# The beginning of a two-layer hybrid trunk kernel: normalized tokens made feature first

## What is computed

```python
def _rms_norm(x, g):
    xf = x.astype(jnp.float32)
    y = xf * lax.rsqrt(jnp.mean(xf * xf, axis=-1, keepdims=True) + EPS)
    return (y * g.astype(jnp.float32)).astype(x.dtype)

def _ada(cond, w, b):
    m = jax.nn.silu(cond) @ w + b
    return jnp.split(m, 3, axis=-1)

def _prologue(x, ctx, c, c_ctx, g, w_mod, b_mod):
    sh, sc, gt = _ada(c, w_mod, b_mod)
    shc, scc, gtc = _ada(c_ctx, w_mod, b_mod)
    hx = _rms_norm(x, g) * (1 + sc[:, None]) + sh[:, None]
    hc = _rms_norm(ctx, g) * (1 + scc) + shc
    h = jnp.concatenate([hc, hx], axis=1)
    return h, gt[:, None], gtc
...
    h, gt, gtc = _prologue(x, ctx, c, c_ctx, norm_g, w_mod, b_mod)
    u, v, g_a, xs, g_b = jnp.split(
        h @ w_in, [A_WIDTH, 2 * A_WIDTH, 3 * A_WIDTH, 3 * A_WIDTH + B_WIDTH], axis=-1)
```

## Time and profile before

| | us |
|---|---|
| median of 3 timed runs | 1304.54 (1301.89 to 1306.85) |
| the profiled execution, device time | 1301.15 |
| the profiled execution, span of the core | 1299.3 |
| PE busy with matmuls | 1223.0 (94%) |
| DVE busy | 851.6 (66%) |
| ACT busy | 518.3 (40%) |
| POOL busy | 445.6 (34%) |

### The profile page before, as it was taken

The page is one execution under the profiler, slowest core; times in us unless marked ns, Lnnn a source line. Parts: engine busy times, 40 slices in busy tenths (PEclk is TensorE's granted clock), DMA queues, the critical chain, the costliest instruction groups (busy, mean ns, idle before and its releaser), DMA issues.

```text
span 1299.3 us, 21119 instructions
## 1 busy us (share of the span) xinstructions
PE 1223.0 (94%) x8508; PEld 1079.1 (83%) x8508; DVE 851.6 (66%) x1494; ACT 518.3 (40%) x956; POOL 445.6 (34%) x358
## 2 busy tenths in 40 slices
PE   1799989999999899999999999999999999999997
PEld 1789878888888848999999998877788888888997
DVE  6697956989925253136484899448877877776125
ACT  6632353320015331034524432146666666665012
POOL 0600000000000003332112212139999888988332
PEclk9899999999999999999999999999999999999999
DMA  9614677425422962103211112330000000000402
GB/s 347 241 66 130 153 209 247 148 81 203 162 90 85 324 231 56 64 33 116 70 44 34 33 66 81 111 100 9 9 17 9 17 9 17 17 9 9 162 28 103
DMA packets 87408, 127.99 MB, mean 99 GB/s; under 512 B 12912, under 2 KB 59376, under 8 KB 86512
## 3 DMA queue, kind: packets, MB, share of 16 engines
q1 hardware_dynamic: 77200, 110.81, 25.8%
q10 hardware_dynamic: 10112, 15.85, 3.5%
HBM read 95.71 MB, written 30.93 MB: 97 GB/s over the span
## 4 chain that ended last, share of the span: by engine, by line
PE 78%; DVE 11%; DMA 4%; ACT 3%; POOL 3%; issue 2%; SPq 0%; ACTq 0%; POOLq 0%; DVEq 0%
PE ps L1732 10%; PE ps L1734 10%; PE ps L1733 10%; PE ps L1743 5%; PE ps L1744 5%; PE ps L1745 5%; PE ps L1986 3%; DVE region_d L1008 3%; PE ps L2020 2%; PE ps L2021 2%; PE ps L2022 2%; PE ps L2006 2%; PE ps L2009 2%; PE ps L2008 2%; PE ps L2007 2%; PE ps L1598 2%
## 5 line engine op out<-in xcount | busy, mean ns | idle before, releaser
L1732 PE MATMUL ps<-w_hi,a_hi 128*128 128x256 f32 x896 | 256.6, 286 | 9.9 <-DVE b_lo L1109 6.3
L1733 PE MATMUL ps<-w_lo,a_hi 128*128 128x256 f32 x896 | 254.9, 284 | 0.0
L1734 PE MATMUL ps<-w_hi,c_lo 128*128 128x256 f32 x736 | 208.2, 283 | 0.0
L601 POOL TENSOR_TENSOR region_b<-region_b,region_d 128x256 f32<-128x256 f32 x40 | 29.7, 749 | 510.0 <-DVE region_d L1412 510.0
L1732 PEld LDWEIGHTS ps<-w_hi,a_hi 128*128 128x128 f32 x896 | 173.2, 193 | 12.2 <-issue 3.7
L1733 PEld LDWEIGHTS ps<-w_lo,a_hi 128*128 128x128 f32 x896 | 173.4, 194 | 0.0
L594 POOL TENSOR_TENSOR w_lo<-weight_ring,w_hi 128x2048 fp32r<-128x2048 f32 x16 | 74.0, 4625 | 199.3 <-ACT w_hi L649 199.3
L1734 PEld LDWEIGHTS ps<-w_hi,c_lo 128*128 128x128 f32 x736 | 141.2, 192 | 0.0
L1743 PE MATMUL ps<-a_hi,w_hi 128*128 128x512 f32 (+1 forms) x384 | 138.6, 361 | 1.4 <-ACT region_d L649 1.4
L1508 DVE TENSOR_REDUCE small<-ps 128x1 f32<-128x1280 f32 x64 | 95.2, 1487 | 65.1 <-PE ps L1986 65.1
L1744 PE MATMUL ps<-b_lo,w_hi 128*128 128x512 f32 (+1 forms) x384 | 136.6, 356 | 0.0
(11 more groups left out here) (225 smaller groups left out, 2940.9 us busy)
## 6 DMA issues: line engine op xcount, KB each, us to landing
weight_ring<-in_w_mod SPq DMA_DIRECT2D x10, 2048.0 KB, 8.5
weight_ring<-in_we_in SPq DMA_DIRECT2D x10, 1024.0 KB, 6.0
weight_ring<-in_wo_in SPq DMA_DIRECT2D x10, 1024.0 KB, 5.2
weight_ring<-cop_t_scratch SPq DMA_DIRECT2D x4, 1536.0 KB, 7.9
region_a<-in_x SPq DMA_DIRECT2D x4, 1024.0 KB, 14.4
region_c<-in_w_mod SPq DMA_DIRECT2D x2, 2048.0 KB, 19.3
bop_scratch<-region_d ACTq DMA_DIRECT2D x16, 256.0 KB, 2.6
cop_t_scratch<-region_d SPq DMA_DIRECT2D x8, 512.0 KB, 7.4
```

The source lines that it names most:

```text
L1732: te.matmul(o, th, wh[:, k], start=k == 0, stop=False)
L1733: te.matmul(o, th, wl[:, k], start=False, stop=False)
L1734: last = te.matmul(o, tl, wh[:, k], start=False, stop=k == last_k)
```

## The change

- The host lays the tokens out a second time, feature first (`xt_in`, 128 x 8 x 1280). They are loaded straight into hT0: chunk 0 in one transfer, chunk 1 in two (features 0 to 511 and 512 to 1023) ahead of the weights; chunk 2 in two, behind the second half of the v weights and the third block of w_mod. The first v weights are now loaded ahead of the second w_mod block, and b_in and c_in by SP's queue and not ACT's. The token-first loads, row scalings, 80 transposes and 24 copies of the beginning are gone.
- ACT squares whole chunks (`feature_squares`) into XQ (region_a). PE sums them over features with one-column matmuls (`token_sums`), ACT takes the root of each chunk apart (`token_root`), DVE refines the reciprocal (`token_rstd`), PE spreads it over all partitions by transposing a broadcast column (`rstd_across`), ACT copies it to rstd_rows (region_d; `rstd_copy`).
- POOL multiplies the tokens of chunks 0 and 1 by rstd_rows (`scale_tokens`, three products of 2048 columns), and, for chunk 2, adds the eight blocks of squares in three halving steps, both ahead of its parameter work.
- Chunk 2 is scaled on DVE together with the modulation (`h_last`), and rounded by ACT in `h_round2`.
- DVE's order is another: the exp of the magnitudes and the parity work behind the sine stand behind the low parts of the first feature half and both weights_rest of v. PE does the lower feature halves of six token tiles for both v halves, then the upper ones; `after_v` and `after_xs` have new places for the state-space work. `weights_rest(("xs", 0))` is ahead of `build_cl(0)`, and the last `mod_evac` of layer 0 behind `weights_rest(("xs", 1))`.
- Some semaphores are shared where there were several.

```diff
-        early = [(M[0], 0), (M[1], 1), (("v", 0), 2), (("v", 1), 0), (M[4], 1), (M[5], 1), (("xs", 0), 1), (("xs", 1), 0),
+        early = [(M[0], 0), (("v", 0), 2), (M[1], 1), (("v", 1), 0), (M[4], 1), (M[5], 1), (("xs", 0), 1), (("xs", 1), 0),
...
-        after_v = {1: [("mods", 4)], 2: [("cols", 4)], 5: [("mods", 5)], 6: [("cols", 5), ("xs", 0)], 7: [("bop", 0)], 8: [("bop", 4)],
-                   9: [("lags", 0)]}
-        after_xs = {0: [("xs", 1)], 2: [("bop", 8)], 4: [("ws", 0)], 5: [("lags", 1)], 6: [("gb", 0), ("bop", 12)], 7: [("vg", 0)],
-                    8: [("vg", 5)]}
+        after_v = {1: [("bc", 2)], 2: [("mods", 4)], 3: [("cols", 4)], 5: [("mods", 5)], 6: [("cols", 5)], 7: [("xs", 0), ("bop", 0)],
+                   9: [("bop", 4)]}
+        after_xs = {1: [("xs", 1)], 2: [("lags", 0)], 4: [("bop", 8)], 5: [("ws", 0)], 7: [("lags", 1)], 8: [("gb", 0), ("bop", 12)],
+                    9: [("vg", 0)], 10: [("vg", 5)]}
...
-            token_loads(X, ld_x)
-            ring_load(*M[0])
-            ring_load(*M[1])
-            ring_load("v", 0)
...
+            feature_load(slice(0, KT), 0, ld_x[0])
+            feature_load(slice(0, 4), 1, ld_x[1])
+            feature_load(slice(4, KT), 1, ld_x[2])
+            ring_load(*M[0])
+            ring_load("v", 0)
+            ring_load(*M[1])
             ring_load("v", 1)
+            off_ring_load(2, s_ld_v)
+            feature_load(slice(0, 4), 2, ld_x[3])
+            feature_load(slice(4, KT), 2, ld_x[4])
+            off_ring_load(3, s_ld_ws)
...
+            def scale_tokens(ks, q, n):
+
+                t0, nt = CHUNKS[q]
+                pool.wait_ge(s_bc_ok, q + 1)
+                z = hT0[:, ks, t0:t0 + nt]
+                g.tensor_tensor(z, z, rstd_rows[:, t0:t0 + nt].unsqueeze(1).broadcast_to([P, n, nt]), ALU.mult).then_inc(s_z, 1)
+
+            scale_tokens(slice(0, KT), 0, KT)
+            scale_tokens(slice(0, 4), 1, 4)
+            scale_tokens(slice(4, KT), 1, 4)
+            t0, nt = CHUNKS[2]
+            pool.wait_ge(s_sq, 5)
+            for i, m in enumerate((4, 2, 1)):
+                a, b = XQ[:, 0:m, t0:t0 + nt], XQ[:, m:2 * m, t0:t0 + nt]
+                g.tensor_tensor(a, a, b, ALU.add).then_inc(s_z, 1)
+                pool.wait_ge(s_z, 4 + i)
...
+            feature_squares(0, slice(0, KT), 0)
+            feature_squares(1, slice(0, 4), 1)
+            token_root(0)
+            feature_squares(2, slice(4, KT), 1)
+            token_root(1)
+            rstd_copy(0)
+            weights_round(("v", 0))
+            mod_row(0)
+            rstd_copy(1)
             mod_row(1)
-            raw_evac(1, (0, 2, 3, 5, 6))
-            weights_round(("v", 0))
-            act.wait_ge(s_h_tr, 16)
             h_round(0, 0)
+            h_round(0, 1)
+            weights_round(("v", 1))
             mod_row(2)
-            h_round(0, 1)
-            raw_evac(2, (0, 2, 3, 5, 6))
-            act.wait_ge(s_h_tr, 24)
+            feature_squares(3, slice(0, 4), 2)
+            feature_squares(4, slice(4, KT), 2)
             mod_row(3)
-            h_round(0, 2)
             h_round(1, 0)
             h_round(1, 1)
-            weights_round(("v", 1))
-            h_round(1, 2)
+            token_root(2)
+            rstd_copy(2)
+            h_round2()
...
+            def h_last(ks):
+
+                t0, nt = CHUNKS[2]
+                if ks[0] == 0:
+                    dve.wait_ge(s_bc_ok, 3)
+                for k in ks:
+                    z = hT0[:, k, t0:t0 + nt]
+                    v.scalar_tensor_tensor(out=z, in0=z, scalar=hA[0][:, k, 0:1], in1=rstd_rows[:, t0:t0 + nt],
+                                           op0=ALU.mult, op1=ALU.mult).then_inc(s_z2, 1)
...
+            def token_sums(q, e):
+
+                t0, nt = CHUNKS[q]
+                for i in range(nt // P):
+                    for k in (range(KT) if e is None else range(4 * e, 4 * e + 4)):
+                        last = te.matmul(sums(q)[:, i:i + 1], XQ[:, k, t0 + P * i:t0 + P * i + P], onec, start=k == 0 and i == 0,
+                                         stop=k == KT - 1 and i == nt // P - 1)
+                return last
```

250 lines of the change are left out of this document (140 added, 110 removed).

## The result

| | before | changed |
|---|---|---|
| median of the timed runs, us | 1305.05 | 1325.43 |
| ratio | | 1.0157, 95% interval 1.0127 to 1.0186 |
| profiled execution, us | 1301.15 | 1327.08 |
| span of the core, us | 1299.3 | 1325.3 |
| first v tile | 48.99 | 54.31 |

The forecast was 1310 (1290 to 1317) with 0.45 for no measurable change. The kernel is slower, and the median lies above the range. Both spans are read in three pieces: the first v tile is 5.3 us later, the stretch from there to the gMLP stage takes 173.3 us and not 155.2, and what lies behind takes 1097.7 and not 1095.1. That is 5.3 + 18.1 + 2.6 = 26.0, the difference of the spans.

A forecast was written before the change was run, and what follows sets the result against it. PE's chain of work bounds the kernel, from when the first v tile runs: 44.0 + 147.5 work + 18.1 holes puts the gMLP stage at 209.6, 5.4 later; 1304.54 + 5.4 = 1310 us, range 1290 to 1317.

The forecast's parts named there:

- The sums: PE's one-column token sums before the first v tile: first 16 from 8.7 to 15.4 us, chunk 1's 16 end at about 21.
- From the roots of chunk 1 to the first v tile: VectorE, held by GpSimd's products, then low parts: first v tile at 44.0 instead of 48.99, 5.0 us gained.
- Rival 3: GpSimd's products with a repeated operand cost 1.5 times 4.6 us: 1320 us; decides from 1.25 on; chance 0.12.
- The holes: PE idle between first v tile and gMLP stage: 18.1 us in sum, against 12.7 for break-even and 7.7 before.
- (a): Low parts of chunks 0 and 1, upper features: GpSimd's halving tree holds VectorE's trigonometry; PE hole of 6.7 us.
- (b): At cols(4): ACT has mod_row(4) behind the eight h_round2, which wait on VectorE; PE hole of 5.4 us.
- (c): Second xs slot: later trigonometry and parameters, build_cl(0) done at 138.4; hole near xs tile 4 of 2.0 us (0 to 4).
- (d): End of xs: both chains 14 us later, the work behind them 5; hole of 4.0 us (2.4 to 6).
- PE's work: PE's busy time between first v tile and gMLP stage: 147.5 us as before; 3.65 removed, 2.3 and 1.4 added.
- "Nothing behind it differs": From the gMLP start on: nothing changes, so a start at 209.6 us gives a span of 1304.7.
- Rivals 1 and 2: GpSimd hardly holds VectorE: 1290 us, chance 0.13; holds it by half: 1294 to 1303, chance 0.17.
- rival 4: At the start: sums and roots could still be the gate despite earlier w_mod; counted in the sum, no chance given.

## Why the prediction was wrong

It summed to a span of 1304.7 and the span was 1325.3, 20.6 us more. (In the medians it is 15.4, 1325.43 for 1310; the rest is where the profiled executions lie among the others.) The direction was right, the size not. By its own steps:

1. **The sums (+10.0 us, the step that failed).** The prediction priced the first 16 at 0.42, "hence some 0.42 each", which was right (0.43), and let the other 32 end "at about 21". They ended at 31.0. The 10.0 us have three parts, and 0.2 in the first 16. First, 1.7 are that the first squares started at 8.35 and not 6.7: chunk 0 was there later than the context tokens of the earlier trace rows, also 1 MB in one transfer (its rows are of 1 KB and not 4, which may be why; no run changes that alone). In other runs with the same loads the sums began at 9.70 to 10.41, so up to 0.7 of it changes from run to run. Second, 2.1 are the prediction's own arithmetic: from 15.4 to 21 there are 5.6 us for 32 sums, 0.18 each, and at the 0.24 that it had for the high level they are 7.7. Third, 6.0 are the clock: the 32 took 13.7 us, and not the 7.7 of the high level. The prediction took it that PE's clock rises once PE is busy, as it did behind the first w_mod block in the earlier trace rows. It didn't within the one-column sums (the runs with a warm start and with 128 columns). The first w_mod block behind them, at 31.48, was still slow. Its bounds for this term, -2.5 to +3 us from a price of 0.12 to 0.30 each, left out the level at which it had itself priced the first 16.
2. **From the roots of chunk 1 to the first v tile (right).** Forecast 21.3 to 44.0, 22.7 us; measured 31.3 to 54.3, 23.0. The holding, the two products of GpSimd, the chain behind, w_lo and half_evac came as written. What was taken differently is which operations are held: the text took one-input operations as free. By the rule of the Trainium skill (SBUF — State Buffer, section Who interferes with whom) a tensor_scalar can hold and be held too, which the text had in a sentence aside. The rows at 32.16 and 38.25 decide for the rule, with 4.45 and 4.52 us. Since the neighbours in each chain have two inputs, it moved the sum by less than 1 us, as the sentence said.
3. **GpSimd's own price (right).** 4.53 and 4.48 us for products with a repeated operand, against 4.6 from the earlier trace rows; the tree 8.53 against 8.1. Rival 3 needed 5.8 or more (1.25 times 4.6).
4. **The holes (right in sum, 19.8 against 18.1).** (a) 5.4 against 6.7; (b) 4.4 against 5.4; (c) 2.4 against 2.0; (d) 2.35 + 1.0 + 3.9 = 7.3 against 4.0, and above the 6 that it had as the upper end. Build_cl was done at 150.4 (forecast 138.4, plus the 10.3 of the late first v tile 148.7).
5. **PE's work (+6.0, a term left out).** 153.5 us against 147.5. The count of matmuls was right, their price was not: each of the holes of 2.4 to 5.4 us in (a) to (c), and the first of (d), is followed by matmuls at the low level. The clock of the three stretches says so (0.89, 0.89 and 0.96), and the window behind the hole of 5.4 us shows one of them:

```profile
84.00:90.00 6.00, 4.67 (x22) 4.67 (x23) 5.79 (x13) 2.40 (x5) 5.12 (x12) 0.50 0.00 0
```

6. **"Nothing behind it differs" (+2.6).** Behind the gMLP start it took 1097.7 and not 1095.1. In the traces of the experiments, with the same code there, this piece was 1095.0 to 1099.1, so 2.6 us are within what it varies by from one execution to the next, and nothing shows a cause.

The first v tile is 10.3 late (10.0 of step 1 and 0.3 of step 2), the holes are 1.7 more (step 4), and 10.3 + 1.7 + 6.0 + 2.6 = 20.6 closes the account. The sign of "the start gains 5 us, the stretch behind loses more" was right for the second half only. Rivals 1 and 2 are out by the rows of the holding, rival 3 by the price; that the sums and roots are the gate (rival 4) was right, but it had been filed as counted already, with no chance and no price of its own. As the likeliest case rested on it, it should have had one: 48 sums at its own 0.42 are 20.2 us, near the 20.6 measured.
